# Merged completion signals and a reordered vector queue in the recurrent scan of a one-core transformer kernel

## The reference, cut to what matters

```python
def _rwkv_step(S, inp):
    r, w, kk, kka, kt, v = inp
    sk = jnp.einsum('bhij,bhj->bhi', S, kk)
    S = S * w[:, :, None, :] - sk[..., None] * kka[:, :, None, :] + v[..., None] * kt[:, :, None, :]
    return S, jnp.einsum('bhij,bhj->bhi', S, r)
```

## Time and profile before

| | |
|---|---|
| time, median of 3 runs | 3879.92 us (3877.7 to 3884.18) |
| the profiled execution's own time | 3877.7 us |
| its span in the trace | 3875.9 us |
| PE busy | 3258.5 us (84%) |
| DVE busy | 1533.0 us (40%) |
| ACT busy | 828.4 us (21%) |
| POOL busy | 273.1 us (7%) |
| the scan in the trace | about 2584 to 3155 us |

### The profile page before, as it was taken

One profiled execution on the slowest core, in us unless ns is written; L12 is line 12 of the kernel. 1 busy time (PEld: TensorE's weight loads), 2 busy tenths in 40 slices (PEclk: granted clock), 3 DMA queues, 4 the chain that ended last, 5 costly groups with the idle time before them and its releaser, 6 DMA issues. The chain is left out here.

```text
span 3875.9 us, 71976 instructions
## 1 busy us (share of the span) xinstructions
PE 3258.5 (84%) x31462; PEld 1890.5 (49%) x31462; DVE 1533.0 (40%) x3373; ACT 828.4 (21%) x1742; POOL 273.1 (7%) x254
## 2 busy tenths in 40 slices
PE   6997989979699897699999669978888837688787
PEld 5845568454344654334343234557777733322222
DVE  3655346562112752321222161157777762311111
ACT  2104211051111641000000100046655421000000
POOL 0000000010000200000000000001222210000000
PEclk9998899997899997799999889979999978799999
DMA  6663136601220112599999801000000012599998
GB/s 172 172 171 105 39 96 171 174 24 61 72 60 30 44 55 109 198 363 343 342 357 342 303 33 65 17 24 4 4 4 4 4 35 109 202 396 399 401 402 348
DMA packets 149196, 605.80 MB, mean 156 GB/s; under 512 B 19232, under 2 KB 22112, under 8 KB 131872
## 3 DMA queue, kind: packets, MB, share of 16 engines
q1 hardware_dynamic: 142560, 579.70, 41.6%
q0 software_dynamic: 6336, 21.63, 2.4%
HBM read 576.52 MB, written 31.07 MB: 157 GB/s over the span
## 5 line engine op out<-in xcount | busy, mean ns | idle before, releaser
L1704 PE MATMUL psum<-ring,big 128*64 128x512 f32 (+1 forms) x6144 | 909.8, 502 | 108.4 <-DMA ring<-moe_w 92.0
L1704 PEld LDWEIGHTS psum<-ring,big 128*64 128x64 f32 (+1 forms) x6144 | 302.7, 125 | 676.1 <-issue 474.7
L371 PE MATMUL psum<-h_uT,ring 128*128 128x264 f32 x1280 | 290.5, 387 | 0.0
L500 DVE SCALAR_TENSOR_TENSOR h_O<-h_O,cond_silu 128x512 f32<-128x512 f32 x336 | 226.8, 744 | 103.3 <-DMA h_O<-ada_w 103.2
L371 PEld LDWEIGHTS psum<-h_uT,ring 128*128 128x128 f32 x1280 | 242.0, 190 | 46.5 <-issue 5.8
L1215 PE MATMUL psum<-ring,big 128*128 128x512 f32 x576 | 249.4, 592 | 2.0 <-PEq L55 2.0
L2257 PE MATMUL psum<-ring,gates 64*64 64x128 f32 (+1 forms) x5120 | 172.6, 258 | 69.7 <-ACT ring L2438 64.5
L1850 DVE TENSOR_TENSOR big<-big,psum 128x512 f32<-128x512 f32 (+1 forms) x48 | 27.3, 596 | 465.4 <-PE psum L1704 465.4
L1985 PE MATMUL psum<-big,ring 128*128 128x512 f32 (+1 forms) x464 | 171.3, 532 | 31.7 <-DVE big L1956 24.0
L2257 PEld LDWEIGHTS psum<-ring,gates 64*64 64x64 f32 x5120 | 135.0, 135 | 85.5 <-DVE ring L2596 75.7
L1858 DVE SCALAR_TENSOR_TENSOR big<-psum,big,gates 64x512 f32<-64x512 f32 (+1 forms) x128 | 78.8, 615 | 244.9 <-PE psum L1704 243.5
(11 more groups left out here) (331 smaller groups left out, 4516.1 us busy)
## 6 DMA issues: line engine op xcount, KB each, us to landing
ring<-moe_w SPq DMA_DIRECT2D x192, 2048.0 KB, 10.6
h_O<-ada_w SPq DMA_DIRECT2D x192, 256.0 KB, 3.0
ring<-w_in SPq DMA_DIRECT2D x16, 2048.0 KB, 14.5
ring<-na_w_qkv SPq DMA_DIRECT2D x6, 2048.0 KB, 7.9
ring<-w_out SPq DMA_DIRECT2D x4, 2048.0 KB, 8.4
bias_rows<-na_table SPq DMA_DIRECT2D x16, 480.0 KB, 15.7
ring<-bias_rows SPq DMA_DIRECT2D x16, 360.0 KB, 3.0
rows<-big SPq DMA_DIRECT2D x10, 512.0 KB, 4.7
```

The lines of the kernel that those rows point to most:

```text
L371: last = nc.tensor.matmul(bank(k, pair_bank(q) + h, NH), w[:, a, f * P:(f + 1) * P], uT[:, a, halves[h]], start=a == 0, stop=a == KD - 1)
L500: nc.vector.scalar_tensor_tensor(into, ada(u), by, into, ALU.mult, ALU.add).then_inc(s.acc, 1)
L1704: last = nc.tensor.matmul(bank(k, b, r.width)[q * r.n:(q + 1) * r.n, :], rowsT[:, half * HALF_K + n, r.first:r.first + r.n], w[:, n, q * r ...
```

## The change

Six edits, all in `rwkv_scan` and its list of signals.

1. The two signals of a level become one. `up` n is gone; `level` n comes after the product into W, and DVE's `step` waits for that. Level 6 has one product and one signal, as before.
2. `step` signals its first addition too (`xa` n), and ACT copies the new N in two halves of 128x256: the first after `xa` n, the second after `x` n.
3. The bonus sums move from bank W(z)+1 to bank U(z)+1, and on PE from ahead of `results` to between `results` and `state`. `low_rank` and one case of `rows` then wait for DVE's `bonus_out`, and `gram_m` waits for rho in its stead.
4. On DVE, rho goes ahead of `state`, `bonus_out` ahead of alpha; `decay` and `learning` become one function (`low_rank`), `key_scale` and `keys` another (`keys`), and both stand ahead of step 2; beta goes ahead of step 5, and the addition of the other half of x0 ahead of step 6.
5. POOL multiplies rates and bonus input ahead of `decayed` and `end`.
6. The event lists follow.

```diff
-        pe=[... "gram_n"] + [f"{x}{n}" for n in range(1, LEVELS) for x in ("up", "level")] + [f"up{LEVELS}"] + ...
+        pe=[... "gram_n"] + [f"level{n}" for n in range(1, LEVELS + 1)] + only("y") + ["state"],
...
             def low_rank(z, t, j, n):
                 if j is not None:
                     after("dve", z, j, "state")
+                if n is not None and lat(n):
+                    made("dve", z, n, "bonus")
...
             def bonus_sum(z, t):
-                    last = nc.tensor.matmul(bank(k, W(z) + 1, 2, SIDE + 2 * i), ...
+                    last = nc.tensor.matmul(bank(k, U(z) + 1, 2, SIDE + 2 * i), ...
             def gram_m(z, t):
-                made("dve", z, t, "bonus" if lat(t) else "beta")
+                made("dve", z, t, "rho" if lat(t) else "beta")
...
             def level(z, t, n):                                  # PE
                 if n < LEVELS - 1:
-                    last = heads(U(z), 0, (m, with_x(z, n % 2 == 0)), width=2 * CH)
+                    heads(U(z), 0, (m, with_x(z, n % 2 == 0)), width=2 * CH)
+                    last = heads(W(z), 0, (n_of(z), m))
+                elif n < LEVELS:
+                    heads(U(z), 0, (m, x_alone(z, n % 2 == 0)))
+                    last = heads(W(z), 0, (n_of(z), m))
                 else:
                     last = heads(U(z), 0, (m, x_alone(z, n % 2 == 0)))
-                ev["pe"][z].done(last, t, f"up{n}")
-                if n < LEVELS:
-                    ev["pe"][z].done(heads(W(z), 0, (n_of(z), m)), t, f"level{n}")
+                ev["pe"][z].done(last, t, f"level{n}")
...
             def slot(z, i, f, y, j, n, m):                       # PE
+                if j is not None:
+                    results(y, j)
                 if n is not None and lat(n):
                     bonus_sum(y, n)
                 if j is not None:
-                    results(y, j)
                     state(y, j)
...
             def level(z, t, n):                                  # ACT
                 if n < LEVELS - 1:
+                    after("dve", z, t, f"xa{n}")
+                    copy(N(z)[:, 0, :, :], woven(U(z), 0)[:, 0, :, :])
                     after("dve", z, t, f"x{n}")
-                    ev["act"][z].done(copy(N(z), woven(U(z), 0)), t, f"N{n}")
+                    ev["act"][z].done(copy(N(z)[:, 1, :, :], woven(U(z), 0)[:, 1, :, :]), t, f"N{n}")
...
             def step(z, t, n):                                   # DVE
-                after("pe", z, t, f"up{n}")
+                after("pe", z, t, f"level{n}")
...
-                tt(x, x, got[:, 0, :, :], ALU.add)
+                ev["dve"][z].done(tt(x, x, got[:, 0, :, :], ALU.add), t, f"xa{n}")
```

More of the change, by code:

```diff
@@ L2109, in scan_events @@
     chain = dict(
-        pe=["gram_m", "raised", "rows", "start", "gram_n"] + [f"{x}{n}" for n in range(1, LEVELS) for x in ("up", "level")]
-            + [f"up{LEVELS}"] + only("y") + ["state"],
+        pe=["gram_m", "raised", "rows", "start", "gram_n"] + [f"level{n}" for n in range(1, LEVELS + 1)] + only("y") + ["state"],
         act=["rows", "x0"] + [f"{x}{n}" for n in range(1, LEVELS - 1) for x in "MN"] + [f"M{LEVELS - 1}"],
-        dve=["mask_m"] + only("mask_ar") + ["mask_b"] + only("mask_br") + ["x0", "mask_n"] + [f"x{n}" for n in range(1, LEVELS + 1)]
+        dve=["mask_m"] + only("mask_ar") + ["mask_b"] + only("mask_br") + ["x0", "mask_n"] + [f"{x}{n}" for n in range(1, LEVELS + 1) for x in ("xa", "x")]
             + only("y", "y_carried") + ["state"],
@@ L2234, in slot @@
             def slot(z, i, f, y, j, n, m):
+                if f is not None:
+                    rates(z, f)
+                    if lat(f):
+                        bonus_in(z, f)
                 if j is not None:
@@ L2238, in slot @@
                     end(y, n)
[L2239 to L2242, removed]
             in_turn(slot)
@@ L2318, in bonus_sum @@
                 for i in range(QUAD):
-                    last = nc.tensor.matmul(bank(k, W(z) + 1, 2, SIDE + 2 * i), own(T_dec, z)[:, i * P:(i + 1) * P], k.head_ones[:, 0:P:CH], start=True, stop=True)
+                    last = nc.tensor.matmul(bank(k, U(z) + 1, 2, SIDE + 2 * i), own(T_dec, z)[:, i * P:(i + 1) * P], k.head_ones[:, 0:P:CH], start=True, stop=True)
                 fr["pe"][z].done(last, t, "bonus")
             def gram_m(z, t):
-                made("dve", z, t, "bonus" if lat(t) else "beta")
+                made("dve", z, t, "rho" if lat(t) else "beta")
                 if lat(t):
@@ L2343, in rows @@
                     after("dve", z, j, "state")
+                    made("dve", z, t, "bonus")
                 for n, src in enumerate((T_beta, T_kappa)):
@@ L2510, in _, with low_rank @@
             tt, stt = nc.vector.tensor_tensor, nc.vector.scalar_tensor_tensor
-            def decay(z, t):
+            def low_rank(z, t):
+                mine = fr["dve"][z]
                 made("pe", z, t, "dec")
-                fr["dve"][z].done(tt(own(T_dec, z), bank(k, U(z)), own(w0, z), ALU.add), t, "dec")
-            def learning(z, t):
-                mine = fr["dve"][z]
+                mine.done(tt(own(T_dec, z), bank(k, U(z)), own(w0, z), ALU.add), t, "dec")
                 made("pe", z, t, "iclr")
@@ L2522, in learning, with keys @@
                 mine.done(tt(pairs(T_rate, z), got, spread(k.a0_cols[:, z * PAIRS:(z + 1) * PAIRS]), ALU.add), t, "iclr")
-            def key_scale(z, t):
+            def keys(z, t):
+                mine = fr["dve"][z]
                 made("act", z, t, "iclr_gate")
@@ L2528, in key_scale @@
                     after("pe", z, t - 1, "gram_n")
-                fr["dve"][z].done(stt(pairs(T_beta, z), pairs(T_rate, z), -1.0, spread(k.ka_cols[:, :]), ALU.add, ALU.mult), t, "m")
-            def keys(z, t):
+                mine.done(stt(pairs(T_beta, z), pairs(T_rate, z), -1.0, spread(k.ka_cols[:, :]), ALU.add, ALU.mult), t, "m")
                 made("dve", z, t, "m")
-                fr["dve"][z].done(stt(pairs(T_beta, z), pairs(T_beta, z), 1.0, tokens(K, z, t), ALU.add, ALU.mult), t, "kt")
+                mine.done(stt(pairs(T_beta, z), pairs(T_beta, z), 1.0, tokens(K, z, t), ALU.add, ALU.mult), t, "kt")
             def alpha(z, t):
@@ L2563, in bonus_out @@
                 made("pe", z, t, "bonus")
-                b, got = bonus[:, place(z, t)[1], :], bank(k, W(z) + 1, PAIRS, SIDE)
+                b, got = bonus[:, place(z, t)[1], :], bank(k, U(z) + 1, PAIRS, SIDE)
                 again = other(z, t, made, "bonus")
@@ L2599, in slot @@
             def slot(z, i, f, y, j, n, m):
+                if j is not None and lat(j):
+                    results(y, j)
+                if n is not None and lat(n):
+                    rho(y, n)
                 if j is not None:
-                    if lat(j):
-                        results(y, j)
                     state(y, j)
+                if n is not None and lat(n):
+                    bonus_out(y, n)
                 if f is not None:
@@ L2608, in slot @@
                     step(z, i, 1)
-                if n is not None and lat(n):
-                    rho(y, n)
-                    bonus_out(y, n)
                 if m is not None:
-                    decay(y, m)
+                    low_rank(y, m)
                 if f is not None:
-                    key_scale(z, f)
-                if m is not None:
-                    learning(y, m)
+                    keys(z, f)
                 if i is not None:
@@ L2628, in slot @@
                 if f is not None:
-                    keys(z, f)
                     kappa(z, f)
@@ L2638, in slot @@
                         masked("mask_br", groups(T_br, y), woven(W(y), 1), k.upto_m, y, n, y)
-                if i is not None:
-                    step(z, i, 5)
                 if f is not None:
@@ L2643, in slot @@
                 if i is not None:
-                    step(z, i, 6)
+                    step(z, i, 5)
                 if n is not None:
@@ L2648, in slot @@
                     ev["dve"][y].done(tt(x, x, bank(k, W(y), SIDE, SIDE).rearrange("p (a x) -> p a x", x=CH), ALU.add), n, "x0")
+                if i is not None:
+                    step(z, i, 6)
+                if n is not None:
                     after("pe", y, n, "gram_n")
```

## The result

The changed kernel took 3939.07 us (median of 4 runs, 3935.78 to 3948.89) against 3882.05 us beside it (3877.7 to 3885.6, 4 runs): ratio 1.0154, 95% interval 1.0136 to 1.0174, some 60 us slower. The forecast was 3946. So the size is known to about +57 to +77 us; it is the kernel before that came out differently on the two occasions, not the changed one.

A forecast was written before the change was run, and what follows sets the result against it. The prediction took a chain through PE, DVE and ACT to bound the scan. Levels 31.0 and borders 35.8 made +66.8 us on 3877.7, so 3944.5, and about 3946 for the median; range 3916 to 3978.

The forecast's parts named there:

- rival A: In the scan PE's clock falls more often, once more every second latent slot: 27 us, 3973; chance 0.15.
- Merged signal, half copies: Each level whose start waits for N: signal +0.46, half copy -0.21, net +0.25 us.
- m and kt: On DVE ahead of step 2, in 21 slots: level 3 starts 4.05 after level 2, not 3.24, +0.81 us.
- The x0 addition: On DVE ahead of step 6, waiting for ACT's `x_first`: 1.28 us at each of 6 borders, 7.7 us.
- L5: Start of level 5 of a slot in the scan; times written after it are us from that start.
- the sum: All terms in the scan: levels 31.0 and borders 35.8, total +66.8 us.
- Results and bonus sums: At 17 borders `results` starts 0.67 later and the bonus sums add 0.98 on the path: 28.1 us.
- POOL's order and beta: POOL's products starting after m, and beta on DVE ahead of step 5: zero cost each.
- Slots: In the scan, slots of context rounds 2.6 us longer, of latent rounds 3.0.
- Rivals B to D: Merged signal free, 3921, chance 0.11; ACT the true bound, 3860, 0.04; no change, 3880, 0.02.

The follow-up runs named there:

- e1: The kernel before with the merged signal alone, N copied whole: ratio 1.0106.
- e2: The kernel before with the two half copies of N alone, up and level signals kept apart: ratio 0.9974.
- e7: The changed kernel with the bonus sums moved back ahead of results: ratio to the kernel before 1.0147.
- the second comparison: The changed kernel measured once more against the kernel before on another occasion: ratio 1.0203, 3940 us against 3863.
- e4: The kernel before with the addition of the other half of x0 moved ahead of step 6, nothing else: ratio 1.0058.
- e10: The changed kernel with three unread products of 16 matmuls in PE's wait for x6 at each border: ratio to the kernel before 1.0228.
- e3: The kernel before with m and kt behind the learning rates and ahead of step 2, nothing else: ratio 1.0061.

## Why the prediction was right

The forecast was +66 us for the median, and about +60 and +77 were measured. It held by its links; the low clock of rival A came beside it, and something that the prediction had passed over took somewhat more away.

*Merged signal, half copies.* Predicted 3.47 from step to step, measured 3.49; +0.46 and -0.21 apart, +0.47 (e1) and -0.19 (e2). The copy of 128x256, taken from another line's row, took 0.38.

*m and kt.* Predicted 2.21 from level 2 to step 2, measured 2.04 (2901.42 to 2903.46), and 4.05 to level 3, measured 3.90 (2905.32). I had taken kt 0.79 behind m from kt and kappa in the earlier trace rows, and its full 0.69 to the end ahead of step 2. It took 0.71 from m to kt and 0.61 from kt to the step. 21 x 0.15 = 3 us too much. The pairs that start 0.60 to 0.61 apart signal a semaphore, too; what the slower pairs have more is a wait of the second for the first.

*The x0 addition.* Predicted step 6 at L5 + 5.56, measured 5.55 (2912.30 to 2917.85). The 4.55 from which it was taken to start in a latent slot was a disturbed one: 4.28 is the value in most slots of either kind. At a border with bonus sums it is the start of `results` that counts, so the sum isn't touched.

*Results and bonus sums.* `results` predicted at L5 + 6.89, measured 6.91. From `results` to the next level 1 the prediction added the 0.98 of the sums; it was 2.80 in the earlier trace rows (2884.91 to 2887.71) and is 3.97 now (2919.21 to 2923.18), 1.17 more, so the term was under-sized by 0.19. Taking the sums out again gives less (e7: 14.0 us in the scan, 0.88 for each), in part because DVE then comes late for step 1. And there are 16 borders with bonus sums and 7 without, not 17 and 6 (eight latent rounds in two directions make 16 sums), which is 0.4 us. POOL's order and beta cost nothing that a run shows; neither was tried alone.

*Slots.* Predicted 2.6 more in a context slot and 3.0 in a latent one. Undisturbed slots of the changed kernel are 23.0 and 26.0 long. Before, the links of an undisturbed context slot make 20.6 (the shortest is 20.7), and the latent slot of the earlier trace rows is followed by the next after 22.9 (level 1 at 2887.71, its own at 2864.78). So +2.4 and +3.1.

*What the sum leaves out.* I took for each link of a slot the shortest that a slot of its kind has, and called the rest disturbance. Over 20 slots, the second to the twenty-first, the undisturbed links grew by 57.8 us, where the prediction's terms make 57.4: kt too much and the way from `results` to level 1 too little are about 3 us each and cancel, and that is luck. The disturbance fell from 24.6 to 18.3 us. That accounts for most of what the scan's 59.4 lacks to 66.8.

*Rival A, the clock.* It had 0.15, and its mechanism is there, in a place that the prediction had not picked out: not spread over the slot but behind the wait for x6, at about every second border, 1.50 us each (3.51 against 2.01), 16.5 us in all for 11. It did not push the time to 3973, since something that the prediction had passed over went the other way: the kernel before had 11.5 us of PE stalls with no releaser in its scan, up to 1.5 each, and some slots up to 4 us longer than their neighbours for the lower clock elsewhere. In the changed kernel such stalls are 0.6 us. The sum has neither of the two: that the forecast came so near the measured time is partly luck, and the second comparison, 17 us apart from the first, says how much.

*Rivals B to D* fall: the signal costs its 0.47 (e1), the half copies of N are worth 0.19 a level (e2) and `x_first` came no earlier for them (2916.89, L5 + 4.59, where it was 4.58), and PE's work doesn't bind, since waits added to the chain lengthened the scan.

What the stalls are is not settled. Three findings point at the supply of PE's instructions: they have no releaser; they go when PE waits once a slot (e4 6.3, changed 0.6) and come back when the wait is filled with other matmuls (e10 24.0, with 2220 more matmul records in the scan); the profile of e10 has 263 packets in the instruction queue, all the others 245. No run changed that supply alone.

## What to carry to other kernels

In a chain that crosses engines, give each product its own signal if its readers differ: one signal for two cost 0.47 us here on every level whose step is on the chain, while the second product, 0.64 to 0.67 long, had lain beside the step. A wait in an in-order queue is charged to what stands behind it, so an operation whose input comes late (x0) goes behind the one on the chain (step 6), even if that leaves work for later. And a copy on the chain can be split so that only its last part follows the last input: 15 us of the scan here, and a ratio of 0.9974. A link read from one slot can hold a stall: compare several slots before pricing it, and ask what the waits that a change adds will hide or bring.

## What the runs showed of the hardware that I had not expected

The granted clock fell to 0.53 in the products behind a wait of 1.60 us, at about half of the borders with the same wait; in e7 it fell at 6 of the 16 borders where that wait was 0.62, and in e3 at level 3 behind PE's wait of up to 2.06, in four context slots. Not every such wait does it: in the changed kernel PE waits 1.46 ahead of level 3, and no stretch at the lower clock begins there. With the wait filled 2 low borders were left of 12. Filling it lost more than it won: PE's stalls without a releaser grew from 1.0 to 24.0 us. On DVE, m to kt, a pair whose second waits for the first's semaphore, took 0.71 from start to start, where neighbours without such a wait take 0.60 to 0.61, and kt to kappa 0.79 in the earlier trace rows.
